# Ten pieces of the input projections placed earlier in TensorE's order

## What is computed

```python
def hybrid_layer(h, ...):
    a = rms_norm(h, attn_norm)
    proj = a @ w_in                       # 24 tiles of 128 columns
    (dq, dk, dv, iq, iw, ik, fq, fk, fv, ff, gq, gk, gv, gg, glr) = split(proj)
    # DSA: an indexer scores all keys, top 128 kept, then attention over those
    dots  = einsum('bqhd,bkd->bqhk', iq, ik) * IDX_DIM ** -0.5
    score = einsum('bqh,bqhk->bqk', iw, relu(dots));  sel = top_k(score, k_top)
    # FoX: attention with forgetting gates;  GLA: gated linear attention in chunks
    mixed = concatenate([o_dsa, o_fox, rms_norm(o_gla) * silu(gg)])
    h = h + mixed @ w_out
    f = rms_norm(h, ffn_norm)
    gate, up = split(f @ w_gate_up)
    return h + (silu(gate) * up) @ w_down

def reference(x, meta_tokens, ...):
    h = concatenate([meta, x])
    for l in range(2):
        h = hybrid_layer(h, ...)
    return h[:, 16:]
```

## Time and profile before

| | |
|---|---|
| median of 3 runs | 1273.12 us (1272.83 to 1273.94) |
| time of the profiled execution | 1273.78 us |
| its span, first to last instruction | 1271.8 us |
| TensorE busy | 1252.4 us, 98% |
| VectorE busy | 926.8 us, 73% |
| ScalarE busy | 661.2 us, 52% |
| GpSimd busy | 289.5 us, 23% |
| granted TensorE clock | 1.00 all through |

### The profile page before, as it was taken

The page is one execution under the profiler, slowest core; times in us unless marked ns, Lnnn a source line. Parts: engine busy times, 40 slices in busy tenths (PEclk is TensorE's granted clock), DMA queues, the critical chain, the costliest instruction groups (busy, mean ns, idle before and its releaser), DMA issues.

```text
span 1271.8 us, 23210 instructions
## 1 busy us (share of the span) xinstructions
PE 1252.4 (98%) x9174; PEld 1184.5 (93%) x9174; DVE 926.8 (73%) x1540; ACT 661.2 (52%) x1100; POOL 289.5 (23%) x168
## 2 busy tenths in 40 slices
PE   7999999999999999999999999999999999999998
PEld 7989999999999999999998889988899999998886
DVE  4598889578999999822236999984889999986100
ACT  5575547655555555622234756386655555554221
POOL 2554313100000000144446462221000000003443
PEclk9999999999999999999999999999999999999999
DMA  5222200132332221233323221100322322213333
GB/s 192 89 64 84 67 34 34 34 116 83 118 115 100 100 100 68 101 100 99 99 83 98 73 84 66 52 35 18 132 99 101 133 101 100 100 67 100 111 104 115
DMA packets 27442, 113.60 MB, mean 89 GB/s; under 512 B 3664, under 2 KB 4304, under 8 KB 21968
## 3 DMA queue, kind: packets, MB, share of 16 engines
q1 hardware_dynamic: 26624, 111.18, 25.3%
q10 hardware_dynamic: 720, 1.09, 0.2%
HBM read 108.79 MB, written 2.10 MB: 87 GB/s over the span
## 4 chain that ended last, share of the span: by engine, by line
PE 89%; DVE 6%; issue 2%; ACT 1%; POOL 1%; DMA 0%; SPq 0%; DVEq 0%; POOLq 0%; ACTq 0%
PE ps L1254 22%; PE ps L868 20%; PE ps L1260 11%; PE ps L874 10%; PE ps L965 5%; PE ps L971 5%; PE ps L966 5%; PE ps L1095 2%; PE ps L1068 1%; PE ps L1078 1%; PE ps L1043 1%; DVE score L1911 1%; PE ps L1152 1%; PE ps L931 1%; PE ps L1110 1%
## 5 line engine op out<-in xcount | busy, mean ns | idle before, releaser
L748 POOL TENSOR_TENSOR wlo<-raw,whi 128x1024 fp32r<-128x1024 f32 x96 | 236.0, 2460 | 917.6 <-ACT whi L1353 637.3
L1353 ACT ACTIVATE whi<-raw 128x1024 fp32r<-128x1024 f32 x116 | 122.6, 1057 | 217.2 <-PE ps L874 174.3
L965 PE MATMUL ps<-xhi,whi 128*128 128x264 f32 (+1 forms) x632 | 177.6, 310 | 0.0
L966 PE MATMUL ps<-xlo,whi 128*128 128x264 f32 (+1 forms) x632 | 171.4, 300 | 0.0
L868 PE MATMUL ps<-hhi,whi 128*128 128x264 f32 (+1 forms) x528 | 157.5, 321 | 0.2 <-DVE hlo L2187 0.2
L868 PE MATMUL ps<-hlo,whi 128*128 128x264 f32 (+1 forms) x528 | 157.6, 321 | 0.0
L965 PEld LDWEIGHTS ps<-xhi,whi 128*128 128x128 f32 x632 | 119.1, 189 | 4.5 <-issue 0.4
L966 PEld LDWEIGHTS ps<-xlo,whi 128*128 128x128 f32 x632 | 119.2, 189 | 3.9
L868 PEld LDWEIGHTS ps<-hhi,whi 128*128 128x128 f32 x528 | 99.4, 188 | 8.1 <-DVE hlo L2187 0.4
L868 PEld LDWEIGHTS ps<-hlo,whi 128*128 128x128 f32 x528 | 99.1, 188 | 7.8
L971 PE MATMUL ps<-xhi,wlo 128*128 128x264 f32 (+1 forms) x632 | 102.4, 304 | 0.0
(11 more groups left out here) (277 smaller groups left out, 3281.5 us busy)
## 6 DMA issues: line engine op xcount, KB each, us to landing
raw<-in_weights SPq DMA_DIRECT2D x116, 512.0 KB, 3.2
raw<-in_groups SPq DMA_DIRECT2D x42, 1024.0 KB, 4.8
out_hT<-h SPq DMA_DIRECT2D x7, 256.0 KB, 4.3
h<-in_hT SPq DMA_DIRECT2D x4, 264.0 KB, 6.2
h<-in_hT ACTq DMA_DIRECT2D x4, 264.0 KB, 5.7
cst<-in_consts SPq DMA_DIRECT2D x1, 780.5 KB, 9.1
xnb<-feat SPq DMA_DIRECT2D x20, 33.2 KB, 2.0
feat<-xnb SPq DMA_DIRECT2D x20, 33.2 KB, 2.0
```

The lines of the kernel that those rows point to most:

```text
L748: nc.gpsimd.tensor_tensor(wlo[:, b], raw[:, b], whi[:, b].bitcast(F32), ALU.subtract).then_inc(split_done, 1)
L965: nc.tensor.matmul(o, whi[:, k % 2, n], xhi[:, n, cut], start=(n == 0), stop=False)
L966: nc.tensor.matmul(o, whi[:, k % 2, n], xlo[:, n, cut], start=False, stop=False)
L1353: return nc.scalar.activation(whi[:, b], raw[:, b], ACT.Copy).then_inc(hi_done, 1)
```

## The change

Only the two strings for TensorE in `STEPS_OF` differ, in seven of their lines. Ten projection pieces stand one to four mixer steps earlier. No instruction is added or removed, the mixer jobs keep their order among themselves and so their banks, the projection pieces keep theirs, and the lists of VectorE, ScalarE, GpSimd and SyncE are the same. The ten:

| layer | piece | now stands before |
|---|---|---|
| 0 | unit 7, half 1, piece 1 | `rope(1)`, `index(3,0)`, `index(3,1)` |
| 0 | unit 10, half 0, piece 2 | `logits` DSA block 0, heads 0 and 1 |
| 0 | unit 11, half 0, piece 0 | a `norm` |
| 0 | unit 12, half 0, piece 1 | `turn_tile(11)`, `meta_values` DSA block 0 |
| 1 | unit 7, piece 1 (512 columns) | `index(1,3)`, `index(2,0)` |
| 1 | unit 8, half 1, piece 0 | a `norm`, `index(3,0)`, `index(3,1)` |
| 1 | unit 10, half 0, piece 1 | a `norm` |
| 1 | unit 11, half 1, piece 1 | `turn` and `logits` DSA block 1 |
| 1 | unit 12, piece 2 (512 columns) | a `norm`, `index(4,1)` |
| 1 | unit 17, half 1, piece 1 | `values`, `turn`, `logits`, `values` |

```diff
 STEPS_OF = (
-    {PE: "AAABAAAAAADAAAAAAAAAAAAAFAAAAAALAAAAAAAAADAMAMAADAMAMAMMAAMMFMMADAAAAAAAAADAAAAPPAAXXAAXAADAAXALAAaA"
-        "ALbAAdAADAAAAAXXXAXXAXAaXAYXAYAbMXAMaAdAMAAAMZYZAXYXZAYXZYXbAAdAAAAZYXZAZAYXALPZAAARRAAPLAYXAYXMAaMa"
+    {PE: "AAABAAAAAADAAAAAAAAAAAAAFAAAAAALAAAAAAAAADAMAMAADAMAMAMMAAMMAFMMDAAAAAAAAADAAAAPPAAAXXAXAAADAXALAAaA"
+         "AALbAdAADAAAAAXXXAXXAXAaXAYXAYAbMXAMaAdAMAAAMZYZAXYXZAYXZYXbAAdAAAAZYXZAZAYXALPZAAARRAAPLAYXAYXMAaMa"
...
-    {PE: "AAAAAABAAADAAAAAAAAAFLAAAAADAAMMAMADAMMAMAFMMAAADMMAAAAADAAAAADAAAAAAXXXAAAYYXAAMMaAMADMAAAAALLAAAXA"
-        "PAAPAAAAZYZYXXAZYXAAAaAAAAAZYXbALAZYXZAAYXZYXZbYXAAMAaARRALMAPPALAAAAAALASTSARATRASTSdRATZYXTZYXZAYX"
+    {PE: "AAAAAABAAADAAAAAAAAAFLAAAAADAAMMAMADAAMMMAFMMAAAADMMAAAAADAAAAAADAAAAAXXXAAAAYYXAMMaAMAADMAAAAALLAAAXA"
+         "PAAPAAAAZYZYXXAZYXAAAaAAAAAZYXbALAAZYXZAYXZYXZbYXAAMAaARRALMAPPALAAAAAALASTSARATRASTSdRATZYXTZYXZAYX"
```

More of the change, by code:

```diff
@@ L232 @@
 STEPS_OF = (
-    {PE: "AAABAAAAAADAAAAAAAAAAAAAFAAAAAALAAAAAAAAADAMAMAADAMAMAMMAAMMFMMADAAAAAAAAADAAAAPPAAXXAAXAADAAXALAAaA"
-        "ALbAAdAADAAAAAXXXAXXAXAaXAYXAYAbMXAMaAdAMAAAMZYZAXYXZAYXZYXbAAdAAAAZYXZAZAYXALPZAAARRAAPLAYXAYXMAaMa"
-        "bAAAdLZZYAXYXZZbYXYAdZYAZZXXYXAAYLXATSARSAaAATRATRASSATTaZbYXAdZDZYXYXAADZYXZbYAdADZAYaAAZDYZAAXXZXb"
-        "AYdXAYXAAaAZYXZYXZYXZbYadZYZYZfZbfdfff",
+    {PE: "AAABAAAAAADAAAAAAAAAAAAAFAAAAAALAAAAAAAAADAMAMAADAMAMAMMAAMMAFMMDAAAAAAAAADAAAAPPAAAXXAXAAADAXALAAaA"
+         "AALbAdAADAAAAAXXXAXXAXAaXAYXAYAbMXAMaAdAMAAAMZYZAXYXZAYXZYXbAAdAAAAZYXZAZAYXALPZAAARRAAPLAYXAYXMAaMa"
+         "bAAAdLZZYAXYXZZbYXYAdZYAZZXXYXAAYLXATSARSAaAATRATRASSATTaZbYXAdZDZYXYXAADZYXZbYAdADZAYaAAZDYZAAXXZXb"
+         "AYdXAYXAAaAZYXZYXZYXZbYadZYZYZfZbfdfff",
      ACTE: "BACDAAAPLAHHICIDAMMCIIDMAMCMMMMMMDJACOADIICJPPIIAPXXDAXXLJaALCeDAJXXXXXXAXaYYXMMaeXAMMYYXYXYePAYXXKY"
@@ L243 @@
      DMAE: "AEEAEAGAAEAEAGAAAAAAAAAAAAAAAAA"},
-    {PE: "AAAAAABAAADAAAAAAAAAFLAAAAADAAMMAMADAMMAMAFMMAAADMMAAAAADAAAAADAAAAAAXXXAAAYYXAAMMaAMADMAAAAALLAAAXA"
-        "PAAPAAAAZYZYXXAZYXAAAaAAAAAZYXbALAZYXZAAYXZYXZbYXAAMAaARRALMAPPALAAAAAALASTSARATRASTSdRATZYXTZYXZAYX"
-        "ZYbXdADadZZAYYXADXZYZbXAYXZYXaZYXZDZYAYXdbXZYXZaZYYdXZbXYdZXYaZXYZXZYXYbDZYZYZaZdbfdffff",
+    {PE: "AAAAAABAAADAAAAAAAAAFLAAAAADAAMMAMADAAMMMAFMMAAAADMMAAAADAAAAAADAAAAAXXXAAAAYYXAMMaAMAADMAAAALLAAAXA"
+         "PAAPAAAAZYZYXXAZYXAAAaAAAAAZYXbALAAZYXZAYXZYXZbYXAAMAaARRALMAPPALAAAAAALASTSARATRASTSdRATZYXTZYXZAYX"
+         "ZYbXdADadZZAYYXADXZYZbXAYXZYXaZYXZDZYAYXdbXZYXZaZYYdXZbXYdZXYaZXYZXZYXYbDZYZYZaZdbfdffff",
      ACTE: "BACADAALPACIIHIDHMMAMCIDAMCMMAMMDMMCIIAJDCIIOADCJAXXXYYJXMaMMADMJALLAPXAPPYYXYXXAaAYPLYXYXYYKXXMaXAL"
```

## The result

The changed kernel takes 1275.15 us (median of 20 runs, 1274.77 to 1276.33), the kernel before 1273.30 us (median of 20, 1272.73 to 1274.46): 1.85 us more, a ratio of 1.0014 with a 95% interval of [1.0008, 1.0020]. The forecast was 1271.9, with a range to 1275.0; the time lies just above it. By the bound of 0.2% that the prediction set this is "no change that can be told"; with 20 runs each it can be told, and it is a loss.

What follows compares the result with a forecast made beforehand. TensorE, 89% of the chain, was taken as the bound, with VectorE as full in layer 1's mixers. Layer 0's 0.7, layer 1's 0.4 and 0.1 for small idle time made 1.2 us: 1271.9 us, range 1268.9 to 1275.0.

Steps and rivals of the forecast that it cites:

- move 1: Layer 0, unit 7: the norm at 72.21 us gains 0.15, lost again at 89.15; 0.6 of wait returns before the norm.
- move 2: Layer 0, unit 10: covers two `logits` gaps, but 1 us becomes a wait before `logits` at 92.03; gain taken as 0.
- move 3: Layer 0, unit 11: the norm's 0.70 wait is covered, but piece 2 needs `wlo`; gain 0.2, new wait 0.4.
- move 4: Layer 0, unit 12, before `turn_tile`: everything behind comes 0.7 us earlier and this passes on; bounds 0 and 1.1.
- Move 5: Layer 1, unit 7: `index(1,3)` comes 1.3 us late, L1911 starts 0.4 late but ends with GpSimd's op; cost 0.
- Moves 6 to 8: Layer 1, brackets of 1.23, 0.67 and 1.02 us: waits for GpSimd or VectorE cut the lead, 0.1 left at `gate`.
- Move 10: Layer 1, unit 17, before `values` at 779.11: `turn` 0.4 us earlier; layer 1 keeps 0.4 in all, 0.1 from before.
- The likeliest case: The whole kernel: 1.2 us of gain, median 1271.9 us, chance 0.50; this case reaches from 0.3 to 2.1 us.
- rival 2: VectorE in layer 1: L1911 or its like escapes a GpSimd collision, winning 2.0 us, to 1269.9; chance 0.18.
- three signs of being wrong: TensorE's rows 2 us or more earlier at 254; L1911's 2.37 turned into 0.4; VectorE over 1 us late at 705.
- The rival on the slow side: Layer 1: late `index(1,3)` reaches VectorE, 1.3 us plus one op held up by 2.0, giving 1275.7; chance 0.10.
- The moved pieces cost: Rival theory set up for the experiments: some moved piece delays a mixer step that mattered; no chance given.

Runs made afterwards that it cites:

- e1: The kernel before with only the four layer 0 pieces moved, layer 1's order as before: 1272.53 us, 0.72 below before.
- e8: The full change without the layer 1 move of unit 7, piece 1 (512 columns): 1275.47 us, 1.93 above before.
- e3: The full change with four small scratch fills on GpSimd in front of its split of unit 15's weights in layer 1: 1271.95 us, ratio 0.9989 to before.
- e7: The full change without the layer 1 move of unit 12, piece 2 (512 columns): 1272.21 us, 1.33 below before.
- e11: The full change with the layer 1 pieces of units 8, 10, 11 and 12 back in their old places: 1272.31 us, 1.09 below before.
- e9: The kernel before with one extra MAX8 on VectorE in front of L1951/L1952 of block 2 in layer 1: 1276.59 us, 3.19 above before.
- e2: The full change without the layer 1 move of unit 11, half 1, piece 1: 1273.07 us, ratio 0.9998 to before.
- e6: The full change with two more pieces (unit 15, half 0, pieces 1 and 2) put before layer 1's second `gate` step: 1274.35 us, ratio 1.0007 to before.
- e4: The kernel before with four small scratch fills on VectorE in front of L1951 of block 2 in layer 1: 1273.26 us, ratio 1.0000.
- e5: The kernel before with twelve small scratch fills on VectorE in front of L1951 of block 2 in layer 1: 1273.45 us, ratio 1.0000.
- e10: The kernel before with one extra MAX8 on VectorE behind L1952 of block 2 in layer 1: 1273.49 us, ratio 1.0002.

## Where the prediction held and where it failed

**Layer 0 held.** Behind the start-up difference of 0.47 us the offsets of the profile after are those of the walk: the norm of move 1 gained 0.13 (predicted 0.15) and waits 0.64 where it was to wait 0.6; `logits` of move 2 waits 0.82 in front of 92 us (predicted about 1) and gains nothing; piece 2 of move 3 waits 0.52 for `wlo` (predicted 0.4) and gains 0.2; behind move 4 everything is 0.72 earlier (predicted 0.7). The rows that answer to the earlier trace rows:

```profile
71.61 0.73 PE L986 MATMUL ps<-sq_parts,ones_r 128*128 128x266 f32 x4 [0.64 <-ACT relu L1545]
...
91.61 0.20 PE L1043 MATMUL ps<-kk,mix_lo 128*16 128x16 f32 x2 [0.82 <-DVE mix_lo L1830]
...
96.85 1.25 PE L971 MATMUL ps<-xhi,wlo 128*128 128x264 f32 x8 [0.52 <-POOL wlo L748]
...
103.72 0.71 PE L1012 MATMUL ps<-cst,feat 128*128 128x128 f32 x5
```

e1 confirms the sum with -0.72.

**Move 5 held, and was better than thought.** `index(1,3)` came 1.3 us late as worked out (701.20 against 701.06 with an offset of -1.19), and the L1911 behind it ended when GpSimd did:

```profile
701.39 2.40 POOL L748 TENSOR_TENSOR wlo<-raw,whi 128x1024 fp32r<-128x1024 f32 x1 [3.74 <-ACT whi L1353]
...
701.97 1.98 DVE L1911 SCALAR_TENSOR_TENSOR score<-relu,w_idx,score 128x144 f32<-128x144 f32 x1 [0.80 <-ACT relu L1545]
```

It started 0.42 later relative to its neighbours, took 0.39 less, and ended where it did against the earlier trace rows. What I missed is small: `index(2,0)` and piece 2 behind it came earlier, and with them ScalarE's next `whi` and GpSimd's next split, to whose end the next L1907 was held. That is the 0.25 us that e8 lacks.

**Moves 6 to 8 held in their own sum.** They give VectorE nothing: its offset is -1.43 from 710 to 755 us. **Move 10** was worth 0.25 to 0.27 where no one was overtaken (e3, e7, e11; predicted 0.3 of its own). In the full change TensorE comes 0.68 nearer to its old times at this place (from 2.05 late at 778 us to 1.37 at 782), but that isn't the move's: e9, which has no moved piece, shows 0.71 there (3.26 to 2.55), time that TensorE had spent waiting for VectorE before. The sum of 1.2 us is what e3, e7 and e11 measured: 1.30, 1.33, 1.09. The likeliest case was right for the versions in which L1952 kept its place and no clock fell. Its exact hit is part luck: the walk had 0 for move 5, which brought 0.25, while it counted 0.1 for moves 5 to 9 and 0.1 for small idle time, of which the runs show nothing.

**The step that failed is one sentence of rival 2,** on the order of a VectorE and a GpSimd instruction: "GpSimd is released by ScalarE, which shifts with TensorE too, so the order of the two mostly stays." The first half is right and is the reason why the second is wrong. GpSimd shifts with TensorE, VectorE did not; I had written a few lines above that what TensorE wins from 701 us on doesn't reach VectorE. When one engine of a close pair follows TensorE and the other doesn't, moving TensorE ahead is what changes their order. I looked at the one pair at 702.74 that had already lost its race, and never listed the pairs that had won theirs by little: L1952 at 756.63 and L748 at 756.91 stood in the trace, 0.28 apart, with a lead of TensorE of up to 0.5 us worked out for that stretch. In the run L748 came 1.78 us earlier and L1952 1.43, L1952 took 2.47 us instead of 0.29, and `gate`, which was to have gained up to 0.8, came 0.72 late. None of the three signs of being wrong appeared, as all three look at other places.

**The rival on the slow side** had the right price for one overtaken op (2.0; it was 2.2), but tied it to the late `index(1,3)`, which cost nothing, and so it got 0.10. That its total (1275.7) is near 1275.15 is luck: 1.3 of it is that delay, which no run shows as a loss, where the runs have the half clock. As "any VectorE op with two SBUF operands that leads a GpSimd op by less than the lead that TensorE wins" it should have had far more. Its second term was missing altogether: the walk counted waits of TensorE at their own length. A wait of 2.33 us cost 1.4 us more on TensorE by the clock behind it, and e2 shows 1.87 us doing the same. In the full change these were worth 1.04 us in the end (e6), and about 1.1 by the executions of e8 and e9 with and without the fall.

**"The moved pieces cost" fell** with e9, which has the whole loss and no move, and with e3, which has all moves and no loss. e8 takes away the piece that did delay a mixer step, by 1.3 us, and the loss stays.

What stays open: why the clock fell in most executions of e8 and e9 and not in all. And the gains of e1, e3, e7 and e11 are of the size of their intervals: that each is 0.7 to 1.3 us rests on the offsets in the traces more than on the medians. These too have their noise: e4, e5, e9 and e10, whose order in layer 0 is that of before, drift by 0.1 to 0.2 us against the same trace between 120 and 180 us.

## What to carry to other kernels

In a kernel where engines run side by side, moving one engine ahead shifts the engines that wait for its buffers and not those that are full themselves. Before an order is changed, list the pairs of a VectorE instruction and a GpSimd instruction that start within a few tenths of each other, where the VectorE one has two SBUF operands or is of a form that the trace shows held elsewhere (L1909 below), and ask for each of the two whether it follows the moved engine: here one flip cost VectorE 2.2 us, nearly the whole length of the GpSimd instruction. And work put in front of a long wait of TensorE pays even when it doesn't bring the awaited result earlier: in e6 it kept the clock.

## What the runs showed of the hardware

- L1952 (two SBUF operands, 0.29 us) takes 2.36 to 2.47 us when it starts 0.07 to 0.18 us behind a GpSimd `tensor_tensor` of 2.40 us, and 0.29 us when it starts 0.12 to 0.87 ahead. Behind L1952 the GpSimd instruction loses little, as little of L1952 is left by then: 2.44 with a lead of 0.12 for VectorE, 2.40 with 0.28. Behind a longer one it loses more: 2.83 and 2.96 behind L1830, of whose 0.70 us 0.55 and 0.69 were left. The Trainium skill ("SBUF — State Buffer", section "Who interferes with whom") says that the one which issues first blocks the other in full; the runs agree in both directions, but for 0.12 to 0.14 us by which the held one ends sooner than the rest of the other and its own time would give. The first of the two pairs with L1830, in the profile before:

```profile
719.07 0.70 DVE L1830 TENSOR_TENSOR mix_hi<-feat,mix_hi 64x528 fp32r<-64x528 f32 x1
719.22 2.83 POOL L748 TENSOR_TENSOR wlo<-raw,whi 128x1024 fp32r<-128x1024 f32 x1 [1.97 <-ACT whi L1353]
```

- One tensor operand alone doesn't make a VectorE instruction safe. A MAX8 takes 0.58 us beside such a split and 0.58 without one (757.71 and 763.75, profile after). But L1909, a TENSOR_SCALAR with one tensor operand and a factor per partition, takes 0.295 us at 695.4 and 2.30 when it starts 0.17 behind the split (profile before).

```profile
757.71 0.58 DVE L1922 MAX8 top<-score 128x8 f32<-128x400 f32 x1
...
762.59 2.40 POOL L748 TENSOR_TENSOR wlo<-raw,whi 128x1024 fp32r<-128x1024 f32 x1 [5.07 <-ACT whi L1353]
...
763.75 0.58 DVE L1922 MAX8 top<-score 128x8 f32<-128x400 f32 x1
```

```profile
59.02 2.38 POOL L748 TENSOR_TENSOR wlo<-raw,whi 128x1024 fp32r<-128x1024 f32 x1 [6.60 <-ACT whi L1353]
59.19 2.30 DVE L1909 TENSOR_SCALAR score<-relu,w_idx 128x144 f32<-128x144 f32 x1
```

- The granted clock of TensorE fell from 1.00 to 0.50 (2.4 to 1.2 GHz) at waits of 2.33 us (the change, e8, e9) and of 1.87 us (e2), and stayed at 1.00 behind those of 0.41 (e6), 0.91 (the change, 733.71), 1.23, 1.38 (e6, 767.48) and 1.51 (e11, 710.44). The fall doesn't stand in one place: in the change and e9 it comes before TensorE goes on; in e2 (0.71 over 734 to 735, the wait over at 733.58) and in e8 (0.98 over 762 to 763, the wait over at 761.71) TensorE had first worked on for 0.8 and 1.2 us at the full clock. And two of the eleven executions of e8 and three of the nine of e9 had no fall. Each of the four lower stretches in the traces is 3.4 us long; in the change TensorE was back at the full clock 3.1 us after it had gone on.
